# RWKV-7 layer of a decode step: token shift, key norms and early turns rearranged, and the scan as an affine recurrence

## What is computed

```python
prev = concatenate([shift0, rw[:, :-1]])          # the token before
xs = rw + (prev - rw) * mu                        # -> r, k, v, xw, xa, xg
w_log = -softplus(-(w0 + tanh(xw) @ w2)) - 0.5;  decay = exp(-exp(w_log))
a = sigmoid(a0 + xa @ a2);  g = sigmoid(xg) @ g2
kk = k * k_k;  kk = kk / max(sqrt(sum(kk * kk over the head)), 1e-12)
k = k * (1 + (a - 1) * k_a)
def step(S, r, w, k, v, a, b):                    # a = -kk, b = kk * a; S is 64 x 64 per head
    S = S * w + (S @ a) b^T + v k^T
    return S, S @ r
```

## Time and profile before

| | us |
|---|---|
| median of three runs | 1956.96 |
| the profiled execution | 1956.52 |
| its span in the trace | 1954.7 |
| operands, pairs, scan (325.1 to 560.6 us) | 235.5 |

### The profile page before, as it was taken

How to read it: one execution, slowest core, us unless ns; L and a number is a source line. 1 busy time by engine, 2 the same in 40 slices (tenths; PEclk the granted TensorE clock), 3 DMA queues, 4 the chain that set the end, 5 groups by cost and what they waited for, 6 DMA issues and landing times.

```text
span 1954.7 us, 42142 instructions
## 1 busy us (share of the span) xinstructions
PE 1807.1 (92%) x19138; PEld 1162.0 (59%) x19138; DVE 685.9 (35%) x1240; ACT 343.6 (18%) x556; POOL 29.7 (2%) x37
## 2 busy tenths in 40 slices
PE   7989994488669999999899999999999999999997
PEld 6956653287449999999683443535344453534444
DVE  4544333762357555375553212110211211021121
ACT  3122320300034333344430000000000000000002
POOL 0010000000000000000000000000000000000000
PEclk9999997676579999999989999999999999999999
DMA  9131532000065444441559999999999999998894
GB/s 291 31 105 40 156 97 34 1 3 2 1 165 151 149 149 137 139 149 47 173 171 417 417 417 416 417 395 417 377 404 401 375 417 364 417 371 324 354 416 172
DMA packets 166439, 463.27 MB, mean 237 GB/s; under 512 B 27770, under 2 KB 110876, under 8 KB 135412
## 3 DMA queue, kind: packets, MB, share of 16 engines
q1 hardware_dynamic: 164910, 457.37, 62.8%
q0 software_dynamic: 1152, 3.15, 0.4%
q10 hardware_dynamic: 198, 0.05, 0.0%
HBM read 451.57 MB, written 8.95 MB: 236 GB/s over the span
## 4 chain that ended last, share of the span: by engine, by line
PE 50%; ACT 1%; DVE 0%; issue 0%; DVEq 0%; ACTq 0%
PE bank L2471 45%; PE bank L2439 1%; PE bank L310 1%; PE bank L312 1%; PE bank L311 1%; PE bank L2323 0%; PE bank L2445 0%; PE bank L2409 0%; PE bank L2402 0%; PE bank L2338 0%; PE bank L2330 0%; ACT ring L2635 0%; PE bank L2342 0%; ACT ring L2634 0%; PE bank L2534 0%; ACT mix_hi L2553 0%
## 5 line engine op out<-in xcount | busy, mean ns | idle before, releaser
L2471 PE MATMUL bank<-ring,x 128*32 128x512 f32 (+1 forms) x6144 | 587.3, 540 | 0.0
L2471 PEld LDWEIGHTS bank<-ring,x 128*32 128x32 f32 x6144 | 195.3, 110 | 358.9 <-issue 356.8
L2471 PE MATMUL bank<-ring,hid 128*32 128x256 f32 x5376 | 291.5, 379 | 0.0
L2471 PEld LDWEIGHTS bank<-ring,hid 128*32 128x32 f32 x5376 | 174.7, 110 | 117.1 <-issue 3.1
L310 PE MATMUL bank<-x_hi,w_hi 128*128 128x320 f32 (+1 forms) x488 | 152.5, 313 | 0.0
L312 PE MATMUL bank<-x_hi,w_lo 128*128 128x320 f32 (+1 forms) x488 | 151.5, 310 | 0.0
L311 PE MATMUL bank<-x_lo,w_hi 128*128 128x320 f32 (+1 forms) x488 | 151.4, 310 | 0.0
L1977 DVE TENSOR_TENSOR w_lo<-ring,w_hi 128x2048 fp32r<-128x2048 f32 (+2 forms) x51 | 112.5, 2208 | 96.7 <-ACT w_hi L1901 96.5
L2835 DVE TENSOR_TENSOR hrow<-sil,bank 128x512 f32<-128x512 f32 (+1 forms) x48 | 26.9, 616 | 297.2 <-PE bank L2471 297.2
L2798 DVE TENSOR_TENSOR xT<-xT,bank 128x320 f32<-128x320 f32 x56 | 23.5, 482 | 277.4 <-PE bank L2439 277.4
L1901 ACT ACTIVATE w_hi<-ring 128x2048 fp32r<-128x2048 f32 (+2 forms) x51 | 94.1, 1848 | 131.4 <-PE bank L312 125.8
(11 more groups left out here) (546 smaller groups left out, 2242.7 us busy)
## 6 DMA issues: line engine op xcount, KB each, us to landing
ring<-in_moe_w_gu SPq DMA_DIRECT2D x128, 1024.0 KB, 15.6
ring<-in_moe_w_down SPq DMA_DIRECT2D x112, 1024.0 KB, 14.2
ring<-in_moe_w_gu SPq DMA_DIRECT2D x128, 768.0 KB, 10.1
ring<-in_ffn_w_gu_even SPq DMA_DIRECT2D x44, 512.0 KB, 4.8
pages<-in_cache_mla SPq DMA_DIRECT2D x128, 144.0 KB, 2.4
ring<-in_w_in_odd SPq DMA_DIRECT2D x12, 1024.0 KB, 5.4
ring<-in_ffn_w_down_even SPq DMA_DIRECT2D x10, 1024.0 KB, 5.1
proj_ring<-in_w_in_even SPq DMA_DIRECT2D x9, 1024.0 KB, 8.4
```

Of the source, the lines that this page charges most:

```text
L2471: mm = t.matmul(ps[banks[g3]][SL * y:SL * y + SL, 0:w], act[:, g3, k, :], m_ring[:, slot, at + y * w:at + (y + 1) * w], start=start, stop= ...
```

## The change

Three parts.

Token shift. ScalarE multiplies the chunks, moved by one token, by `mu` (`shifted`), VectorE adds (1 - mu) times the chunk (`mix`), in four groups in the order of need: xw, xa and xg; k; r; v. Columns at a sequence's start are written by VectorE from the stored shift.

Key norms and turns. The head sums are taken with tokens on partitions (24 small instructions into one bank), clamped, rooted and inverted on 128 x 24 values, spread to 64 columns a head by ScalarE (`rx`), and turned back by TensorE into four banks, from which VectorE multiplies. v is turned right after the low-rank products and copied by ScalarE. The gate's four copies go to ScalarE. The order of the exponentials changes. The states' turns use four banks and wait for the gate's copies, not for the operands; b's and k's six groups of turns use four banks, copied by VectorE and ScalarE in turn.

Scan. With `W = XT . A` and `U0 = XT . (KM V)` for all chunks at once (`AV`, `WU`), a chunk is affine in its start state: `S(c+1) = (P(c) S(c) + Q(c)) * decay` with `P = I + B W` and `Q = B U0 + K V`, and `y(c) = (r + W BM) . S(c) + own terms`. `transitions` forms P and the changed r, `own_terms` forms Q and the part of y without the state, `step` and `from_state` are the eight matmuls of 64 x 64 that depend on S(c), and `advance` is VectorE's add and multiply. The first chunk starts from zero and needs no step. The samples' work (`spread`, `new_states`, `new_state`) is laid between the chunks. The final nine groups of turns use four banks, copied by ScalarE and VectorE in turn. The DMAs are the same.

The diff, cut to its core:

```diff
+    def mix(g):
+        cs = GROUPS[g]
+        v.wait_ge(tmp_ready, g + 1)
+        dv(v, v.tensor_copy(dif[:, cs.start:cs.stop, SEQ:TOK:DS], shT[:, cs.start:cs.stop, :]))
+        for c in cs:
+            last = v.scalar_tensor_tensor(out=rwT[:, c, :], in0=rwT[:, c, :], scalar=omu[:, c:c + 1], in1=dif[:, c, :],
+                                          op0=ALU.mult, op1=ALU.add)
+        last.then_inc(mixed, 1)
+    mix(0)
+    mix(1)
...
+    v.tensor_scalar(rn[:, 0:2, :], ps[4][:, 0:2 * RH].rearrange("p (i h) -> p i h", i=2), 1e-24, None, ALU.max)
+    v.tensor_scalar(rn[0:64, 2, :], ps[4][0:64, 2 * RH:3 * RH], 1e-24, None, ALU.max).then_inc(kk_var, 1)
...
+    v.wait_ge(kk_root, 1)
+    v.reciprocal(rn[:, 0:2, :], rn[:, 0:2, :])
+    v.reciprocal(rn[0:64, 2, :], rn[0:64, 2, :]).then_inc(rn_ready, 1)
...
-    dv(v, v.reciprocal(t2, t2))
-    dv(v, v.tensor_tensor(kk, kk, t2, ALU.mult))
...
+        v.wait_ge(bc_full, c + 1)
+        last = v.tensor_tensor(kk[:, c, :], kk[:, c, :], ps[4 + c][:, 0:TOK], ALU.mult)
...
+    def shifted(g):
+        for c in GROUPS[g]:
+            last = s.activation(dif[:, c, 1:TOK], rwT[:, c, 0:TOK - 1], ACT.Copy, scale=V("rwkv_mu", c))
+        last.then_inc(tmp_ready, 1)
+    shifted(0)
+    shifted(1)
+    s.wait_ge(mixed, 1)
     s.activation(tw[:, :], rwT[0:64, 12, :], ACT.Tanh).then_inc(tg_ready, 1)
+    shifted(2)
+    shifted(3)
...
+    for i in range(3):
+        s.wait_ge(v_full, i + 1)
+        r = TILES[i][1]
+        s.activation(rowV[0:r, i, :], ps[5 + i][0:r, :], ACT.Copy).then_inc(v_taken, 1)
+    s.wait_ge(rn_ready, 1)
+    for i in range(3):
+        r = TILES[i][1]
+        s.activation(rx[0:r, i, :, :], rn[0:r, i, :].rearrange("p (h o) -> p h o", o=1).to_broadcast([r, RH, RD]), ACT.Copy).then_inc(rx_ready, 1)
...
+    t.wait_ge(mixed, 4)
+    for i, (lo, r) in enumerate(TILES):
+        for c in range(4):
+            mm = t.transpose(ps[5 + i][0:r, c * P:(c + 1) * P], vT[:, c, lo:lo + r], C("ident"))
+        mm.then_inc(v_full, 1)
+    t.wait_ge(tg_ready, 2)
+    for c in range(4):
+        t.wait_ge(lo_act, 5 + c)
+        t.matmul(ps[c][:, 0:TOK], g2[:, c * P:(c + 1) * P], sg[:, :], start=True, stop=True).then_inc(lo_full, 1)
...
+    t.wait_ge(v_taken, 3)
+    for c in range(4):
+        for i, (lo, r) in enumerate(TILES):
+            if c == 0:
+                t.wait_ge(rx_ready, i + 1)
+            mm = t.transpose(ps[4 + c][:, lo:lo + r], rx[0:r, i, 2 * c:2 * c + 2, :].rearrange("p h d -> p (h d)"), C("ident", r, 0, r))
+        mm.then_inc(bc_full, 1)
...
+    for n in range(6):
         lo, r = TILES[n % 3]
-        if n >= 2:
-            t.wait_ge(row_free, n - 1)
-        src = (bF, kF, rwT)[n // 3]
+        if n < 4:
+            t.wait_ge(st_free, n + 5)
+        else:
+            t.wait_ge(row_act if n % 2 else row_dve, n // 2 - 1)
         for c in range(4):
-            mm = t.transpose(ps[n % 2][0:r, c * P:(c + 1) * P], src[:, (8 if n >= 6 else 0) + c, lo:lo + r], C("ident"))
+            if n % 3 == 0:
+                t.wait_ge(b_ready if n < 3 else k_ready, c + 1)
+            mm = t.transpose(ps[n % 4][0:r, c * P:(c + 1) * P], (bF, kF)[n // 3][:, c, lo:lo + r], C("ident"))
...
+    def transitions(cs):
+        for pr in range(4):
+            for c in cs:
+                for h in (2 * pr, 2 * pr + 1):
+                    hs, _, cols = head(h)
+                    js, i = block_of(c), c // 2
+                    t.matmul(ps[P_BANK[c]][hs, pr * RD:(pr + 1) * RD], WU[js, i, h, 0, :], rowB[js, i, cols], start=True, stop=True)
+                    mm = t.matmul(ps[P_BANK[c]][hs, 256 + pr * RD:256 + (pr + 1) * RD], WU[js, i, h, 0, :], BM[js, i, h, 1, :],
+                                  start=True, stop=True)
+        mm.then_inc(p_full, 1)
+    def own_terms(cs):
+        for pr in range(4):
+            for c in cs:
+                for h in (2 * pr, 2 * pr + 1):
+                    hs, _, cols = head(h)
+                    js, i = block_of(c), c // 2
+                    out = ps[Q_BANK[c]][hs, pr * RD:(pr + 1) * RD]
+                    t.matmul(out, rowB[js, i, cols], WU[js, i, h, 1, :], start=True, stop=False)
+                    t.matmul(out, rowK[js, i, cols], rowV[js, i, cols], start=False, stop=True)
+                    out = ps[Q_BANK[c]][hs, 256 + pr * RD:256 + (pr + 1) * RD]
+                    t.matmul(out, WU[js, i, h, 1, :], BM[js, i, h, 1, :], start=True, stop=False)
+                    mm = t.matmul(out, rowV[js, i, cols], KM[js, i, h, 1, :], start=False, stop=True)
+        mm.then_inc(q_full, 1)
+    def step(c):
+        t.wait_ge(s_ready, c)
         for h in range(RH):
+            hs, pr, _ = head(h)
+            mm = t.matmul(ps[7][hs, pr * RD:(pr + 1) * RD], PT[hs, c, pr, :], ST[hs, c, pr, :], start=True, stop=True)
+        mm.then_inc(s_full, 1)
+    def from_state(c):
+        for h in range(RH):
+            hs, pr, _ = head(h)
+            at = 256 * (c % 2) + pr * RD
+            mm = t.matmul(ps[2 + c // 2][hs, at:at + RD], ST[hs, c, pr, :], AR[hs, pr, 1, chunk(c)], start=True, stop=True)
+        mm.then_inc(y_full, 1)
+    def new_states(hs_):
+        for h in hs_:
             h0, pr = 64 * (h % 2), h // 2
...
+            t.wait_ge(blk_ready, h + 1)
+            if h % 2 == 0 and pr >= 2:
+                t.wait_ge(n_ready, pr - 1)
+            out = ps[pr % 2][h0:h0 + 64, :]
+            t.matmul(out, rowB[0:64, 2, h * RD:(h + 1) * RD], ub[:, h % 2, :, :].rearrange("p b v -> p (b v)"), start=True, stop=False)
+            mm = t.matmul(out, rowK[0:64, 2, h * RD:(h + 1) * RD], vb[:, h % 2, :, :].rearrange("p b v -> p (b v)"), start=False, stop=True)
+            mm.then_inc(n_full, 1)
...
+    for i in range(2):
+        for pr in range(4):
+            mm = t.transpose(ps[i][:, pr * P:(pr + 1) * P], AR[:, pr, 0, P * i:P * (i + 1)], C("ident"))
+        mm.then_inc(a_full, 1)
         for h in range(RH):
...
+            for c in (2 * i, 2 * i + 1):
+                js, cols = block_of(c), slice(h * RD, (h + 1) * RD)
+                mm = t.matmul(ps[2 + i][js, cols], KM[js, i, h, 0, :], rowV[js, i, cols], start=True, stop=True)
         mm.then_inc(r_full, 1)
...
+    for h in range(RH):
+        hs, pr, _ = head(h)
+        out = ps[5 + h % 2][hs, pr * P:(pr + 1) * P].rearrange("p (a t) -> p a t", a=2)
+        for b in range(NB):
+            mm = t.matmul(out[:, :, b * DS:(b + 1) * DS], S0T[hs, b, pr, :],
+                          AR[hs, pr, :, SEQ + b * DS:SEQ + (b + 1) * DS], start=True, stop=True)
+    mm.then_inc(sy_full, 1)
     for h in range(RH):
         mm = t.matmul(ps[7][0:64, h * RD:(h + 1) * RD], KM[0:64, 2, h, 0, :], rowV[0:64, 2, h * RD:(h + 1) * RD], start=True, stop=True)
     mm.then_inc(mv_full, 1)
+    t.wait_ge(a_ready, 2)
+    for i in range(2):
+        t.wait_ge(r_ready, i + 1)
+        for half in range(2):
+            for h in range(4 * half, 4 * half + 4):
+                for c in (2 * i, 2 * i + 1):
+                    js = block_of(c)
+                    mm = t.matmul(ps[2 * i + half][js, (h % 4) * P:(h % 4 + 1) * P].rearrange("p (a v) -> p a v", a=2), XT[js, i, h, :], AV[js, i, h, :, :],
+                                  start=True, stop=True)
+            mm.then_inc(w_full, 1)
+        if i == 0:
+            t.wait_ge(sy_ready, 2)
+            for pr in range(4):
+                mm = t.transpose(ps[4][0:64, pr * P:(pr + 1) * P], SY[:, pr, 0, :], C("ident"))
+            mm.then_inc(tr_full, 1)
+    t.wait_ge(wu_act, 1)
+    t.wait_ge(wu_dve, 1)
+    own_terms((0, 1))
+    transitions((1,))
+    t.wait_ge(wu_act, 2)
+    t.wait_ge(wu_dve, 2)
+    transitions((2, 3))
     t.wait_ge(r2_ready, 1)
     for h in range(RH):
...
+        mm = t.matmul(ps[4][0:64, h * RD:(h + 1) * RD], XT[0:64, 2, h, :], rhs2[:, h * RD:(h + 1) * RD], start=True, stop=True)
     mm.then_inc(u2_full, 1)
+    t.wait_ge(p_ready, 1)
+    own_terms((2, 3))
+    step(1)
+    t.wait_ge(p_ready, 2)
+    from_state(1)
+    t.wait_ge(q_dve, 1)
     t.wait_ge(u2_ready, 1)
     for h in range(RH):
...
+        hs, pr, cols = head(h)
+        out = ps[5][hs, pr * 64:(pr + 1) * 64]
+        t.matmul(out, U2[:, cols], BM[0:64, 2, h, 1, :], start=True, stop=False)
+        mm = t.matmul(out, rowV[0:64, 2, cols], KM[0:64, 2, h, 1, :], start=False, stop=True)
     mm.then_inc(y2_full, 1)
...
+    step(2)
+    from_state(2)
+    t.wait_ge(q_dve, 2)
+    t.wait_ge(q_act, 2)
+    new_states((0, 1))
+    step(3)
+    from_state(3)
+    new_states(range(2, RH))
...
+    def taken(c):
+        i = c // 2
+        v.tensor_tensor(PT[:, c, :, :], four(P_BANK[c], 0), C("ident64").rearrange("p (o t) -> p o t", o=1).to_broadcast([P, 4, RD]), ALU.add)
+        return v.tensor_tensor(AR[:, :, 1, chunk(c)], four(P_BANK[c], 256), AR[:, :, 1, chunk(c)], ALU.add)
+    def decayed(c):
+        return wend[:, :, c:c + 1].to_broadcast([P, 4, RD])
+    def advance(c):
+        v.wait_ge(s_full, c)
+        if c % 2:
```

(51 more changed lines are left out.)

308 lines of the change are left out of this document (122 added, 186 removed).

## The result

The changed kernel takes 1886.37 us (median of four runs, 1879.04 to 1890.77) against 1954.83 for the kernel before on the same chip: a ratio of 0.964, with a 95% interval from 0.960 to 0.968. The forecast was 1905, with 1886 as the lower end of its range. The gain is 68 us where 52 were worked out. The profiled execution is the slowest of the four: 1890.77 us, its span 1888.9.

What follows compares the result with a forecast made beforehand. No engine bounds the three RWKV stages: waits in chains and TensorE's low clock do, and their losses pass one for one to the kernel. 1956.5 - 28 (operands) - 24 (scan) = 1904.5, so 1905 us; range 1886 to 1919.

Steps and rivals of the forecast that it cites:

- Operands: Stage before the pairs: last copy at 376.3 (low clock) or 366.4 (high) instead of 399.5; the middle, -28 us.
- The wait that it does name: Operands: VectorE stands before the small inverse with the k path queued behind it, 1.2 us at the low clock.
- The fourth rival: Operands: norms come back as late as today because ScalarE's queue holds them; only -16 there, 1917 us; chance 0.06.
- The first rival: Operands: TensorE's clock stays low throughout; -23 us there, 1910 us in all; chance 0.18.
- Pairs and tail: Stage before the scan unchanged at 48.4 us (bounds -4 and +2); tail after the final turns stays at 12.8 us.
- Scan: First instruction to final turns, 99.7 us before: -24 us at the low clock, bounds -15 and -40.
- The low-clock sum: Scan: its groups of work added up at TensorE's low clock, ending with the last new state at 76.0 us.
- the four changes between full and half array: Scan's start: TensorE loses 0.3 us at each of four switches between full-array and half-array work, an estimate.
- Its main price: Scan: small matmuls alternating halves in runs of 8 take 0.057 us an instruction, bounds 0.053 and 0.107.
- The third rival: Scan: halves don't overlap in runs of 8; own terms 13.7 us each instead of 7.2, 1918 us; chance 0.07.
- The second rival: Scan: clock rises when the own terms start; the part from 26 to 76 takes 34 us, 1889; chance 0.22.
- fifth rival: Experts' loop: rounding moves a token, one expert exceeds 96 and a ninth pass of 113 us runs, 2018 us; chance 0.03.

Runs made afterwards that it cites:

- scan_all_paused: Changed kernel with 16 pauses of TensorE in the new scan, each waiting for a ScalarE copy of 1024 columns: 1932.8 us.
- the paused one: Changed kernel with six pauses of TensorE inside the scan's two groups of own terms, each waiting for a ScalarE copy: 1902.56 us, scan 14.9 us longer.

## Why the prediction was right, and where it was wrong

**Operands: right.** -28 forecast, -30.6 measured, inside the bounds of 23 and 33. Step by step: squares at 12 us, measured 11.1. The 24 instructions of 128 loaded columns took 4.52 us, 0.19 each where I had 0.12: 1.6 too few. They were not hidden: the low-rank products, for which ScalarE and then VectorE waited, started right behind them, at 15.6 us where I had 15.3. That the path held is in part luck, as the squares came about 1 us early. I had VectorE free 16.6 us into the stage (341.7) and decay's sigmoids done at 20.7 at the low clock (345.8); the running sum began at 20.8, behind a wait of 4.88 for ScalarE. My own times put a wait of 4.1 us there, which the text doesn't name. The wait that it does name, 1.2 us ahead of the small inverse, didn't come: VectorE's inverse at 357.94 follows its work before it without a gap. The small inverses took 0.39, against 0.35. Twelve turns of b began 37.9 us into the stage, and the last copy ended at 43.8, where I had 41.3 (high) and 51.2 (low) and took the middle. Undoing a step cost 6.2, 8.0 and 12.4 us, where the expectations before those runs had 7 to 10, 5 to 8 and 11 to 13. The six groups of turns took 5.9 us from 370.63 to the last copy's end, 0.99 each where I had 1.05, but that agreement is luck: b's three groups took 1.53 together, and then TensorE stood 2.22 us, since VectorE's first copies were queued behind its `bonus` product (until 374.2). The fourth rival (norms late, -16) didn't happen.

**The clock in the operands** rose for parts of the stage: 0.65 in the mean, 30 us of 44 low. The first rival, low throughout, gave -23 and fell, though the clock stayed low until 359.1.

**Pairs and tail: right.** 0 and 0.1 us, where I had 0 for both. ScalarE and VectorE share the final copies now, and SyncE's nine issues still follow one another, from 481.6 to 488.6.

**Scan: the mechanism right, the size wrong.** -24 forecast, -45.0 measured. TensorE has no wait over 1 us from the stage's start to the second step, as expected. The low-clock sum held: 76.0 against 73.4 to 79.1 by scan_all_paused. One of its terms didn't: the four changes between full and half array, 0.3 us each by my estimate, cost nothing; each of these groups in the changed kernel (at 1.00) starts before the one ahead has ended, and those in scan_all_paused (at 0.50) do too. Its main price held. At the low clock the eight instructions of a head's own terms (four matmuls) take 0.49 us; these rows of scan_all_paused are the same instruction of two heads that follow one another:

```profile
460.11 0.31 PE L1562 MATMUL bank<-BM,WU 64*64 64x64 f32 x1
...
460.60 0.31 PE L1562 MATMUL bank<-BM,WU 64*64 64x64 f32 x1
```

That is 0.061 each, and I had 0.057 with bounds of 0.053 and 0.107. The third rival, no overlap in runs of eight instructions and 13.7 us for a group, fell. The samples' products, which come in runs of sixteen, were priced at 0.07 from a row whose clock was 0.62 in the mean, and cost 0.085 at the low clock.

What failed is the choice of clock, in the step "the clock rises in the scan". I gave it 0.22 and took the low clock for the forecast, 76 us; the scan ran 33 of its 54.6 us at 1.00, which is about 21 (19 to 24.5) of its 45 us and nearly all by which it beat my 24. For the rise I had that 30 us were dense, against it one stretch of 4 us at 0.50 in a burst. That stretch said nothing on 30 dense us. The nearer row was the one of the pairs, the same form of matmul, kept dense, at 1.00. The second rival's price was 1889 with the part from 26 to 76 us taking 34; its -40 was 5 short, since the stage's first 5.5 us ran at 1.00 too, and the clock was up again from 441.0, 16 us into the stage and during W, and not only from the own terms on. I had also named 50 to 60 us to the final turns for this case, and 54.6 came. The dense stretches of the changed kernel, first from the samples' products to the first third of W, then the rest of W, then own terms:

```profile
430.70:441.00 10.30, 10.30 (x124) 10.30 (x124) 0.00 (x0) 1.43 (x3) 0.00 (x0) 0.50 0.01 2
441.00:444.00 3.00, 3.00 (x49) 2.63 (x46) 1.28 (x2) 0.95 (x2) 0.00 (x0) 1.00 0.00 0
444.10:448.10 4.00, 4.00 (x115) 4.00 (x112) 1.28 (x2) 0.00 (x0) 0.00 (x0) 1.00 0.01 4
```

For 10.3 us the samples' products and what follows them kept TensorE busy at 0.50, and then it went to 1.00. So density alone didn't decide it: the same products alternating between the halves stayed at 1.00, and more than that no run shows. 115 instructions of own terms in 4.0 us are 0.035 each. A group of 128 took 4.7 where I had 7.2 at the low clock. The clock fell again only at 468.3, when the samples' states led.

Six rows of TensorE's matmuls that follow one another in the timeline of the own terms (the weight loads between them are left out):

```profile
444.29 0.22 PE L1552 MATMUL bank<-BM,WU 64*64 64x64 f32 x1
...
444.29 0.27 PE L1549 MATMUL bank<-WU,rowB 64*64 64x64 f32 x1
444.35 0.22 PE L1552 MATMUL bank<-BM,WU 64*64 64x64 f32 x1
...
444.40 0.22 PE L1549 MATMUL bank<-WU,rowB 64*64 64x64 f32 x1
...
444.40 0.22 PE L1553 MATMUL bank<-KM,rowV 64*64 64x64 f32 x1
...
444.46 0.22 PE L1550 MATMUL bank<-rowV,rowK 64*64 64x64 f32 x1
```

A head's order in the program is L1549, L1550, L1552, L1553, and then the next head's L1549. Here the next head's L1549 starts ahead of the L1553 of the one before: the two halves run side by side. The Trainium skill, "TensorE: Matmul & The Clock Gate", Part 3, has matmuls start and end in strict program order; for the start, these rows disagree (the ends are modelled in this profile).

**The final turns and the clock.** Two windows of the changed kernel, both with nothing but turns on TensorE since 479.9:

```profile
481.90:485.30 3.40, 3.40 (x18) 2.82 (x17) 1.35 (x3) 1.18 (x2) 0.00 (x0) 0.50 0.68 105
485.30:488.80 3.50, 1.35 (x12) 1.08 (x10) 1.31 (x2) 1.18 (x2) 0.00 (x0) 0.99 1.00 155
```

After dense turns the clock is at 1.00, as in the earlier trace rows. The same page's Part 4 says of TensorE's transpose mode that it doesn't count as busy for the clock. If these turns are in that mode, which no run here shows, the clock would have stayed at 0.50 by that rule, and two traces disagree.

**The whole.** -30.6 and -45.0 are 75.6; 7.5 us came back ahead of the operands and 2.1 behind the tail, which the profiled execution lost and the change doesn't touch. The median gain is 68. The stages after the scan stay within the 3 us I allowed; the one ahead of the operands didn't. The ninth pass of the experts (fifth rival) didn't happen: L2471 is L2623 now, with the same 6144 and 5376 instructions as in the earlier trace rows.

## What to carry to other kernels

Where a dependent chain is replaced by dense work, work out the time at both levels of the clock, and choose by the row whose work is most like the new one in form, length and density, not by a short burst; where no such row settles it, give both times their due chance. A stage with waits can cost twice: 18 us of the old scan and 8 of the paused one were no wait, but the clock after it. Small matmuls into one half of the array are worth alternating between the halves; here one by one beat runs of 16 instructions by over a third, and nothing between the two was tried on the same product.
